# Expert value table of a PEER layer: half of its columns gathered, half streamed through a full weight matrix

## The chip, the cores and the metric

One NeuronCore of a Trainium2 chip runs the whole program. The metric is the time of one launch on the device in microseconds. Engines are named as in the profile: PE (TensorE), DVE (VectorE), ACT (ScalarE), POOL (GpSimd), SP (SyncE).

## What is computed

A layer of a streaming encoder for 256 tokens of width 2048: a token-mixing sub-layer (state-space branch and latent attention), then the PEER sub-layer, which the change is about. For each token and each of 8 heads, 16 of 16,384 experts are chosen; expert e is row e of `peer_u` and row e of `peer_v`, 2048 float32 (8 KB) each.

```python
q = jnp.dot(h, w_q).reshape(b, s, PEER_HEADS, 2, PEER_HALF)
s1 = jnp.einsum('bshd,kd->bshk', q[:, :, :, 0], keys_1)   # 128 keys
s2 = jnp.einsum('bshd,kd->bshk', q[:, :, :, 1], keys_2)
v1, i1 = lax.top_k(s1, PEER_TOPK)                         # 16
v2, i2 = lax.top_k(s2, PEER_TOPK)
# top 16 of the 16 x 16 sums; expert = i1 * 128 + i2; gate = softmax
u = jnp.take(u_table, e_blk, axis=0)
act = jax.nn.gelu(jnp.einsum('td,ted->te', h_blk, u), approximate=False)
v = jnp.take(v_table, e_blk, axis=0)
return jnp.einsum('te,ted->td', g_blk * act, v)
```

The result is scaled by `1 + gate2`, added to `ALPHA * x1` and normalised.

## The kernel before

The 256 tokens are two blocks of 128 tokens, one token on each partition. Up to about 1625 us of the trace the program streams weight matrices from SP through TensorE; in the last of these stages (`wq`, lines 1787 to 1817) DVE also finds the experts of head 0 of block 0 (`top_sides`, `top_pairs`, `top_experts`, lines 1756 to 1785). Then comes the stage `all`, the rest of the program.

Its unit is a group: one head of one block, 16 in all. A group has 32 gathers, 16 of `peer_u` and then 16 of `peer_v`. One gather (line 1993) is an indirect DMA that POOL issues: it fetches one table row for each of the 128 tokens, 128 x 8 KB or 1.05 MB, into one of the 8 slots of `rrow`. Row r goes to slot r mod 8, and POOL issues it once the user of row r - 8 is done with it (`row_used`, `row_used_pe`). All 32 gathers of a group wait for `expert_ready`, which DVE raises when it has written the group's 16 indices in `eid` (line 1784).

On DVE the order within a group (line 1832 on) is written out by hand:

```python
for e in range(TOPK):                 # 16 rows of peer_u: dots
    row = use_row(r0, e, i_sem)
    last = V.tensor_tensor_reduce(row, row, h2[:, b, :], ...)
top_sides(head + 1); top_pairs(1 - k); top_experts(1 - k)   # experts of the NEXT group
# gate, gelu -> wgt; 4 diagonal matrices for TensorE
# 12 rows of peer_v: ps += row * wgt      (4 rows go to TensorE)
```

So the experts of group g + 1 are found between the u rows and the v rows of group g. ACT supplies `gex` (exponential, line 1257) and `gel` (gelu, line 1267). The v rows are summed in PSUM: 12 of 16 by DVE into `ps` (line 1859), 4 of 16 by TensorE (line 929) as a matmul of a diagonal weight matrix `diag` with the row into `aux`. After 8 groups a block is finished (lines 1873 to 1880: both sums, gate, residual, layer norm) and stored by SP (line 541); block 1 follows.

Of the kernel before, what the change touches and what calls it, by code (L numbers as in the profile page):

```python
# [15 lines left out]
ds = bass.ds  # L16
# [42 lines left out]


# [24 lines left out]
def constants():  # L85

    c = np.zeros((P, C_ALL), np.float32)
# [9 lines left out]
    c[:, C_EPS] = EPS  # L97
    return c
# [29 lines left out]
def build(nc, a, out, stop="all"):  # L128
    ctx = ExitStack()
    with ctx:  # L130
# [49 lines left out]
        gate1, shift2, scale2, gate2 = (adabc[:, j, :] for j in range(4))  # L180
# [80 lines left out]
        ln2 = at("ln2", 174 * KB, [P, 2, D])  # L261
# [15 lines left out]
        tsel = pk("tsel", 6, [P, 2, TOPK])  # L277
        tval = pk("tval", 7, [P, 2, TOPK])
        eidf = pk("eidf", 8, [P, TOPK])
        eid = pk("eid", 9, [P, 2, TOPK], U32)  # L280
# [5 lines left out]
        wgt = pk("wgt", 15, [P, 2, TOPK])  # L286
        diag = acc[:, 0, :].rearrange("p (j n k) -> p j n k", j=2, n=2)
        fin = at("fin", 192 * KB, [P, D])
# [111 lines left out]
        diag_ready = sem("diag_ready")  # L400
        row_used_pe = sem("row_used_pe")
        sums_read = sem("sums_read")
        ln2_in = sem("ln2_in")
# [24 lines left out]
        ada_rows = nc.dram_tensor("ada_rows", (1, ADA_ALL * W), F32, kind="Internal").ap()  # L428

# [13 lines left out]


        PE_ROWS = tuple(TOPK + e for e in (3, 7, 11, 15))
        NPE, NDVE = len(PE_ROWS), 2 * TOPK - len(PE_ROWS)

        def rows_done(r, pe):

            n = r // (2 * TOPK) * NPE + sum(x <= r % (2 * TOPK) for x in PE_ROWS)  # L450
            return n if pe else r + 1 - n
# [5 lines left out]
        def _(sp_):  # L457
# [11 lines left out]
            sp_.dma_start(con[:, :], a["consts"]).then_inc(con_in, 16)  # L469
# [67 lines left out]
            if on("all"):  # L537
                for b in range(BLK):

                    sp_.wait_ge(fin_ready, b + 1)  # L540
                    sp_.dma_start(out[0, b * P:(b + 1) * P, :], fin[:, :]).then_inc(out_done, 16)
                sp_.wait_ge(out_done, 16 * BLK)
# [3 lines left out]
        def _(pe):  # L546
# [49 lines left out]
            pe.sem_inc(row_used_pe, NPE)  # L596
# [316 lines left out]
            if on("all"):  # L913
                pe.wait_ge(score_a, 4)
                pe.wait_ge(score_v, 4)
                for b in range(BLK):
                    if b:
                        pe.wait_ge(sums_read, 1)

                    def pair(i, first):  # L920
                        for k in range(2):
                            head = PEER_HEADS * b + k
                            for j, x in enumerate(PE_ROWS):
                                r = head * 2 * TOPK + x
                                pe.wait_ge(diag_ready, i * 4 + (head * 2 + j // 2 + 1))
                                pe.wait_ge(row_full[r % ROWS],
                                           i * (16 * 4 * TOPK // ROWS) + 16 * (r // ROWS + 1))
                                for n in range(4):
                                    last = mm(aux[:, n, :], diag[:, j // 2, j % 2, :],  # L929
                                              rrow[:, r % ROWS, n * W:n * W + W], start=(first and k == 0 and j == 0),  # L930
                                              stop=False, skip_group_check=True)
                                last.then_inc(row_used_pe, 1)

                    pair(0, True)
                    with pe.Fori(1, 4) as i:
                        pair(i, False)
# [3 lines left out]
        def _(act):  # L940
# [272 lines left out]
            if on("h2"):  # L1213
# [12 lines left out]
                for b in range(BLK):  # L1226
                    for q in range(4):
# [3 lines left out]
                            .then_inc(h2_hi_ready, 1)  # L1231
            if on("wq"):
# [16 lines left out]
            if on("all"):  # L1249

                act.wait_ge(score_v, 4)
                act.wait_ge(score_a, 4)
                for b in range(BLK):

                    def gate(n_expr, k):
                        act.wait_ge(top_ready, n_expr)
                        F(gex[:, k, :], tval[:, k, :], ACT.Exp, bias=ngm[:, k:k + 1], accum_out=gsum[:, k:k + 1])\
                            .then_inc(gate_exp, 1)

                    if b == 0:  # L1260
                        gate(1, 0)

                    def pair(i, last_one):
                        for k in range(2):

                            act.wait_ge(row_used, i * (2 * NDVE) + (ROWS + (PEER_HEADS * b + k) * NDVE + TOPK))
                            F(gel[:, k, :], dots[:, k, :], ACT.Gelu).then_inc(gelu_ready, 1)  # L1267
                            if not (last_one and k == 1):
                                gate(i * 2 + (PEER_HEADS * b + k + 2), 1 - k)

                    with act.Fori(0, 4 - b) as i:
                        pair(i, False)
                    if b:
                        pair(3, True)
                    norm_root(b + 5)
# [3 lines left out]
        def _(dve):  # L1279
# [412 lines left out]
            if on("mix"):  # L1692
# [5 lines left out]
                dve.wait_ge(ada_in_ready, 16 * 4)  # L1698
# [39 lines left out]
            if on("wq"):  # L1738
# [32 lines left out]
                def top_experts(k):  # L1771
# [5 lines left out]
                    for s in range(2):  # L1777
# [4 lines left out]
                        link(V.tensor_reduce(tsel[:, s, :], onehot[:, :, :], AX_X, ALU.add))  # L1782
                    link(V.scalar_tensor_tensor(eidf[:, :], tsel[:, 0, :], float(KEYS), tsel[:, 1, :], ALU.mult, ALU.add))
                    V.tensor_copy(eid[:, k, :], eidf[:, :]).then_inc(expert_ready, 1)  # L1784
                    V.tensor_scalar(ngm[:, k:k + 1], tval[:, k, 0:1], -1.0, None, ALU.mult).then_inc(top_ready, 1)

                def use_row(r0, e, n_trip):

                    r = r0 + e
                    dve.wait_ge(row_full[r % ROWS], n_trip * (16 * 4 * TOPK // ROWS) + 16 * (r // ROWS + 1))  # L1790
# [9 lines left out]
                for s in range(4):  # L1800
                    for q in range(4):
# [10 lines left out]
                        if (s, q) == (3, 0):  # L1812
                            top_experts(0)
# [4 lines left out]
            if on("all"):  # L1818
                dve.wait_ge(ln2_in, 32)
                dve.wait_ge(qT_a, 4)  # L1820
                for b in range(BLK):
                    link(V.memset(psf, 0.0))
                    dve.wait_ge(score_a, 4)
                    base = b * PEER_HEADS * 2 * TOPK

                    def pair(i, last_one, i_sem):
                        for k in range(2):
                            r0 = base + k * 2 * TOPK

                            for e in range(TOPK):  # L1830
                                row = use_row(r0, e, i_sem)
# [14 lines left out]
                            head = PEER_HEADS * b + k  # L1846
                            for j in range(2):

                                dve.wait_ge(row_used_pe, i_sem * (2 * NPE) + (NPE + head * NPE - 2 + 2 * j))
                                for n in range(2):  # L1850
# [193 lines left out]
```

## Time and profile before

| | us |
|---|---|
| median of 3 runs | 3003.13 |
| lowest, highest | 2998.79, 3005.52 |
| the profiled execution | 3004.59 |
| its span, first to last instruction | 3002.7 |
| DVE busy | 2353.8 (78%) |
| PE busy | 1807.9 (60%) |
| POOL busy | 961.5 (32%) |
| DMA queue q0 (gathers and others from POOL) | 614.51 MB, 50.9% of 16 engines' span |

The page divides the span in 40 slices of 75 us. The stage `all` takes slices 22 to 40. Durations below come from the profiled execution. In a row of the groups, the first number after the bar is the busy time in us, then the mean of one in ns, then the idle time before them with what ended it. "DMA share" is the mean busy share of the 16 DMA engines.

### The profile page before, as it was taken

What the parts mean: (1) busy time and instruction counts of PE and PEld (TensorE: products, weight loads), DVE (VectorE), ACT (ScalarE), POOL (GpSimd) and SP (SyncE); (2) the same over time, 40 slices, a digit from 0 to 9 for tenths busy, and PEclk for the clock granted to TensorE, in tenths of its full rate; (3) what the DMA queues carried; (4) which work ended last, traced back from release to release, by engine and by line L of the source; (5) the groups of instructions that cost most, each with busy time, mean ns of one, the idle gap of its engine ahead of it and who ended that gap; (6) DMA issues with size and microseconds to landing.
All of it is one profiled execution on the core that took longest, in us unless ns stands there. A gap on an engine that the chain in (4) does not pass through costs nothing.

```text
span 3002.7 us, 31625 instructions
## 1 busy us (share of the span) xinstructions
PE 1807.9 (60%) x10880; PEld 1498.1 (50%) x10880; DVE 2353.8 (78%) x2564; ACT 683.0 (23%) x712; POOL 961.5 (32%) x727
## 2 busy tenths in 40 slices
PE   4689999999999999998886223212122222212322
PEld 3589998888888889997786111001001110000111
DVE  7757677788877874444657999998999989989997
ACT  1144442344444444333342000000000000000000
POOL 0000011222222220000003555655663555556652
PEclk9799999999999999999988665565665655556556
DMA  8746568655555554655536999999998999999996
GB/s 339 285 173 214 205 222 299 223 209 203 207 207 197 196 189 177 239 182 210 182 141 244 386 402 403 403 397 400 420 400 321 380 403 393 403 404 400 398 404 265
DMA packets 135095, 880.07 MB, mean 293 GB/s; under 512 B 15416, under 2 KB 20144, under 8 KB 36944
## 3 DMA queue, kind: packets, MB, share of 16 engines
q0 software_dynamic: 93600, 614.51, 50.9%
q1 hardware_dynamic: 39792, 263.69, 24.2%
q8 instruction: 66, 1.08, 0.1%
q10 hardware_dynamic: 1600, 0.49, 0.1%
q14 instruction: 37, 0.30, 0.0%
HBM read 876.50 MB, written 2.13 MB: 293 GB/s over the span
## 4 chain that ended last, share of the span: by engine, by line
PE 40%; DVE 27%; DMA 14%; issue 10%; POOL 5%; ACT 3%; DVEq 0%; ACTq 0%; POOLq 0%
DMA rrow<-in_peer_u,eid 10%; PE ps L585 9%; DVE ps L1859 9%; PE ps L587 9%; PE ps L586 9%; POOL rrow L1993 5%; DVE rrow L1832 3%; DMA rrow<-in_peer_v,eid 3%; DVE wlo L1288 2%; ACT whi L949 2%; PE ps L565 2%; DVE acc L1337 2%; PE ps L567 2%; PE ps L566 2%; PE aux L929 1%
## 5 line engine op out<-in xcount | busy, mean ns | idle before, releaser
L929 PE MATMUL aux<-rrow,acc 128*128 128x512 f32 x512 | 337.0, 825 | 1018.7 <-DVE acc L1852 774.6
L1288 DVE TENSOR_TENSOR wlo<-raw,whi 128x2048 fp32r<-128x2048 f32 x216 | 510.7, 2366 | 374.2 <-ACT whi L949 365.4
L929 PEld LDWEIGHTS aux<-rrow,acc 128*128 128x128 f32 x512 | 133.8, 272 | 1221.3 <-issue 971.3
L1832 DVE CUSTOM_DVE_ANT_0 rrow<-rrow,h 128x2048 f32<-128x2048 f32 x256 | 584.0, 2292 | 61.0 <-DMA rrow<-in_peer_u,eid 52.4
L949 ACT ACTIVATE whi<-raw 128x2048 fp32r<-128x2048 f32 x216 | 412.8, 1913 | 704.6 <-PE ps L587 478.6
L1993 POOL DMA_INDIRECT rrow<-in_peer_u,eid x256 | 416.5, 1627 | 310.2 <-DVE eid L1784 90.3
L1993 POOL DMA_INDIRECT rrow<-in_peer_v,eid x256 | 356.0, 1391 | 358.0 <-DVE ps L1859 292.3
L1859 DVE SCALAR_TENSOR_TENSOR ps<-rrow,wgt,ps 128x2048 f32<-128x2048 f32 x192 | 452.2, 2355 | 14.4 <-DMA rrow<-in_peer_v,eid 6.8
L585 PE MATMUL ps<-h_hi,whi 128*128 128x256 f32 (+1 forms) x1568 | 453.3, 289 | 5.8 <-DVE wlo L1288 4.4
L587 PE MATMUL ps<-h_hi,wlo 128*128 128x256 f32 (+1 forms) x1568 | 443.5, 283 | 0.0
L586 PE MATMUL ps<-h_lo,whi 128*128 128x256 f32 (+1 forms) x1568 | 443.5, 283 | 0.0
L1898 POOL DMA_DIRECT2D ada_in<-in_p_ada x128 | 69.3, 541 | 749.1 <-DVEq L1438 599.8
L585 PEld LDWEIGHTS ps<-h_hi,whi 128*128 128x128 f32 (+1 forms) x1568 | 299.1, 191 | 18.9 <-issue 10.5
L586 PEld LDWEIGHTS ps<-h_lo,whi 128*128 128x128 f32 (+1 forms) x1568 | 299.1, 191 | 4.0 <-issue 3.8
L587 PEld LDWEIGHTS ps<-h_hi,wlo 128*128 128x128 f32 (+1 forms) x1568 | 299.0, 191 | 0.0
L1267 ACT ACTIVATE gel<-dots 128x16 f32<-128x16 f32 x16 | 3.4, 216 | 1048.9 <-DVE dots L1832 1048.9
L1337 DVE SCALAR_TENSOR_TENSOR acc<-ada_in,csil,acc 128x512 f32<-128x512 f32 x240 | 205.6, 857 | 20.0 <-DMA ada_in<-in_p_ada 5.9
L565 PE MATMUL ps<-whi,h_hi 128*128 128x512 f32 x320 | 135.9, 425 | 54.1 <-DVE wlo L1288 54.1
L585 PE MATMUL ps<-yT_hi,whi 128*128 128x256 f32 x512 | 144.9, 283 | 0.0
L586 PE MATMUL ps<-yT_lo,whi 128*128 128x256 f32 x512 | 144.9, 283 | 0.0
L587 PE MATMUL ps<-yT_hi,wlo 128*128 128x256 f32 x512 | 144.9, 283 | 0.0
L566 PE MATMUL ps<-whi,h_lo 128*128 128x512 f32 x320 | 131.6, 411 | 0.0
(312 smaller groups left out, 3056.5 us busy)
## 6 DMA issues: line engine op xcount, KB each, us to landing
raw<-in_p_in SPq DMA_DIRECT2D x104, 1024.0 KB, 4.9
ada_in<-in_p_ada POOLq DMA_DIRECT2D x128, 512.0 KB, 5.2
ada_in<-in_p_ada SPq DMA_DIRECT2D x32, 1024.0 KB, 9.7
raw<-in_p_so SPq DMA_DIRECT2D x32, 1024.0 KB, 4.9
raw<-in_p_mo SPq DMA_DIRECT2D x16, 1024.0 KB, 7.1
raw<-in_p_bc SPq DMA_DIRECT2D x16, 1024.0 KB, 4.9
raw<-in_p_mix SPq DMA_DIRECT2D x16, 1024.0 KB, 4.9
raw<-in_p_pq SPq DMA_DIRECT2D x16, 1024.0 KB, 4.8
```

The source lines that it names most:

```text
L565: mm(outs[b], x_hi[:, k, t], hi[:, kc, 0:width], start=(k == 0), stop=False)
L566: mm(outs[b], x_lo[:, k, t], hi[:, kc, 0:width], start=False, stop=False)
L585: mm(o, wh, x_hi[:, k, :], start=(k == 0 and first), stop=False, skip_group_check=True)
L586: mm(o, wh, x_lo[:, k, :], start=False, stop=False, skip_group_check=True)
L587: last = mm(o, wl, x_hi[:, k, :], start=False, stop=(k == klast), skip_group_check=True)
L929: last = mm(aux[:, n, :], diag[:, j // 2, j % 2, :], rrow[:, r % ROWS, n * W:n * W + W], start=(first and k == 0 and j == 0), stop=False, ...
L949: F(whi[:, n % 2, :, 0:cols_], raw[:, n % 4, :, 0:cols_], ACT.Copy).then_inc(hi_ready, 1)
L1288: V.tensor_tensor(wlo[:, n % 2, :, 0:cols_], raw[:, n % 4, :, 0:cols_], whi[:, n % 2, :, 0:cols_].bitcast(F32), ALU.subtract).then_inc(lo_ ...
L1337: last = V.scalar_tensor_tensor(acc_, tile[:, kc, :], csil[:, k:k + 1], acc_, ALU.mult, ALU.add)
L1832: last = V.tensor_tensor_reduce(row, row, h2[:, b, :], 1.0, 0.0, ALU.mult, ALU.add, dots[:, k, e:e + 1])
L1859: V.scalar_tensor_tensor(psf, row, wgt[:, k, e:e + 1], psf, ALU.mult, ALU.add)\
L1993: G.indirect_dma_start(out=rrow[:, r % ROWS, :], out_offset=None, in_=a[table][0], in_offset=bass.IndirectOffsetOnAxis(ap=eid[:, k, e:e + ...
```

## The change

The stage `all` is split in two passes over all 16 groups, and the 2048 columns of `peer_v` in two halves.

* Pass 1 (before.py's loop, `pair`) handles only `peer_u`: 16 rows of a group, then the experts of the next group, then the weights of this group, into a table `w_all` of 256 columns that keeps all weights. The indices go to `eid_all`, the two key numbers of each expert to `sides`.
* Columns 1024 to 2047 of `peer_v` (input `p_vg`, laid out apart) are gathered in a second pass: 256 gathers of 128 x 4 KB, each added by DVE into `ps` (`add_row`). There are 8 slots `vrow`. None of them goes to TensorE.
* Columns 0 to 1023 (input `p_vd`) are not gathered. A matrix of weights is built with one column per expert for every token: `wt[b][k1, k2, t]`, 128 x 128 x 128 float32 for each block, which holds the weight where token t has chosen expert (k1, k2) and zero elsewhere. For each token it is the product of two one-hot matrices over the token's 128 selections, one of them scaled by the weights: 32 steps of 4 tokens per block. The one-hots of block 0 are made by ACT during the second half of pass 1 (`one_hots`), those of block 1 by DVE after pass 1, each step followed by one `add_row`. ACT copies each product from PSUM to `wt` (`weights_out`).
* Then the whole left half of the table is read by SP in 64 units of 1.05 MB through 4 buffers (`vden`), 8 float32 matmuls of 128x512 each, into `aux`.
* Both blocks are finished together at the end. `x1`, whose place the matrices take, is stored in DRAM (ACT's queue) and read back, with gate2 and the last norm's rows. The loads of `ln2` leave the start of the stage, and one of four broadcast loads of `adabc` is replaced by a small one.

```diff
@@ DVE, pass 1
                             if not (last_one and k == 1):
-                                top_sides(i * 2 + (PEER_HEADS * b + k + 1))
+                                top_sides(group + 1)
                                 top_pairs(1 - k)
-                                top_experts(1 - k)
+                                top_experts(1 - k, group + 1)
...
-                            link(V.scalar_tensor_tensor(wgt[:, k, :], gel[:, k, :], st[:, 48 + k:49 + k],
-                                                        gex[:, k, :], ALU.mult, ALU.mult))
...
-                            for n, e in enumerate(mine):
-                                row = use_row(r0 + TOPK, e, i_sem)
...
-                                V.scalar_tensor_tensor(psf, row, wgt[:, k, e:e + 1], psf, ALU.mult, ALU.add)\
-                                    .then_inc(row_used, 1)
+                            V.scalar_tensor_tensor(w_all[:, ds(group * TOPK, TOPK)], gel[:, k, :], st[:, 48 + k:49 + k],
+                                                   gex[:, k, :], ALU.mult, ALU.mult).then_inc(w_ready, 1)
@@ DVE, after pass 1
+                for n in range(OHB):
+                    if n >= 2:
+                        dve.wait_ge(wt_done, OHB + n - 1)
+                    o = oh[1][:, n % 2]
+                    t4 = slice(n * OHT, n * OHT + OHT)
+                    link(V.tensor_tensor(o, niota.unsqueeze(1).unsqueeze(1).broadcast_to([P, 2, OHT, P]),
+                                         selT[:, 0:2, t4].unsqueeze(3).broadcast_to([P, 2, OHT, P]), ALU.is_equal))
+                    V.tensor_tensor(o[:, 1], o[:, 1], selT[:, 2, t4].unsqueeze(2).broadcast_to([P, OHT, P]), ALU.mult)\
+                        .then_inc(oh_ready, 1)
+                    add_row(n)
+                for r in range(OHB, BLK * SEL):
+                    add_row(r)
@@ POOL
+                for r in range(BLK * SEL):
+                    if r % TOPK == 0:
+                        pool.wait_ge(expert_ready, r // TOPK + 1)
...
+                    pool.wait_ge(row_used, r + 1)
+                    gather(rrow[:, r % ROWS, :], a["peer_u"][0], r).then_inc(row_full[r % ROWS], 16)
+                for r in range(BLK * SEL):
+                    if r < ROWS:
...
+                        pool.wait_ge(row_used, ROWS + BLK * SEL - ROWS + r // 2 + 1)
+                    else:
+                        pool.wait_ge(vrow_used, r - ROWS + 1)
+                    gather(vrow[:, r % ROWS, :], a["p_vg"], r).then_inc(vrow_full[r % ROWS], 16)
@@ SP
+                for u in range(NVU):
+                    if u < 4:
...
+                        sp_.wait_ge(row_used, ROWS + BLK * SEL - 4 + u + 1)
+                    else:
+                        sp_.wait_ge(vden_used, u - 3)
+                    if u == 3:
...
+                        sp_.wait_ge(wt_done, BLK * OHB)
+                    sp_.dma_start(vden[:, u % 4], a["p_vd"][u * P:(u + 1) * P, :].rearrange("p (q n) -> p q n", q=2))\
+                        .then_inc(vden_full[u % 4], 16)
@@ PE
+                pe.wait_ge(wt_read, BLK * OHB)
+                for u in range(NVU):
+                    pe.wait_ge(vden_full[u % 4], vden_before[u % 4] + 16 * (u // 4 + 1))
+                    for q in range(2):
+                        for b in range(BLK):
+                            for n in range(DV // W):
+                                last = mm(aux[:, 2 * b + n, :], wt_column(b, 2 * u + q),
+                                          vden[:, u % 4, q, n * W:n * W + W],
+                                          start=(u == 0 and q == 0), stop=(u == NVU - 1 and q == 1))
+                    last.then_inc(vden_used, 1)
```

How the instructions stand in the program. First DVE at the border of the last two groups, before (`eid` gets the indices, `ps` the sums; "ISA" with `dots` is one u row):

```order
L1782 TENSOR_REDUCE tsel<-onehot 128x16
L1783 SCALAR_TENSOR_TENSOR eidf<-tsel 128x16
L1784 CAST eid<-eidf 128x16
L1785 TENSOR_SCALAR ngm<-tval 128x1
L1841 RECIPROCAL st<-gsum 128x1
L1843 SCALAR_TENSOR_TENSOR wgt<-gel,st,gex 128x16
L1852 TENSOR_SCALAR acc<-con,wgt 128x128 x4
L1859 SCALAR_TENSOR_TENSOR ps<-rrow,wgt,ps 128x2048 x12
L1832 ISA rrow,dots<-rrow,h_72 128x2048
L1832 ISA dots 128x1
```

Between the indices and the next group's first u row stand 12 v rows. The same place of the change (`acc` is now the store of `eid_all` and `w_all`):

```order
L1884 TENSOR_REDUCE sides<-onehot 128x16
L1885 SCALAR_TENSOR_TENSOR eidf<-sides 128x16
L1887 CAST acc<-eidf 128x16
L1888 TENSOR_SCALAR ngm<-tval 128x1
L1939 RECIPROCAL st<-gsum 128x1
L1941 SCALAR_TENSOR_TENSOR acc<-gel,st,gex 128x16
L1930 ISA rrow,dots<-rrow,h_72 128x2048
L1930 ISA dots 128x1
```

The v rows are gone from there: the u rows that need the indices of line 1887 come next. They stand behind the last group, on DVE, where the one-hots of block 1 (`oh`) begin:

```order
L1939 RECIPROCAL st<-gsum 128x1
L1941 SCALAR_TENSOR_TENSOR acc<-gel,st,gex 128x16
L1973 TENSOR_TENSOR oh_165<-cos_60,selT 128x1024
L1975 TENSOR_TENSOR oh_165<-oh_165,selT 128x512
L1957 TENSOR_SCALAR ps<-vrow,acc 128x1024
L1973 TENSOR_TENSOR oh_165<-cos_60,selT 128x1024
L1975 TENSOR_TENSOR oh_165<-oh_165,selT 128x512
L1960 SCALAR_TENSOR_TENSOR ps<-vrow,acc,ps 128x1024
```

Each v row is now 1024 wide, and the first 32 of 256 alternate with one step of one-hots each.

## Rows read from the trace of the kernel before

**Rows 1.** The page: the span in 40 equal slices (75 us each).
```profile
DVE  7757677788877874444657999998999989989997
...
DMA  8746568655555554655536999999998999999996
```

**Rows 2.** The page: costliest groups of instructions, with idle before them.
```profile
L1832 DVE CUSTOM_DVE_ANT_0 rrow<-rrow,h 128x2048 f32<-128x2048 f32 x256 | 584.0, 2292 | 61.0 <-DMA rrow<-in_peer_u,eid 52.4 <-issue 8.1 <-DVE ps L1822 0.5
...
L1993 POOL DMA_INDIRECT rrow<-in_peer_v,eid x256 | 356.0, 1391 | 358.0 <-DVE ps L1859 292.3
L1859 DVE SCALAR_TENSOR_TENSOR ps<-rrow,wgt,ps 128x2048 f32<-128x2048 f32 x192 | 452.2, 2355 | 14.4 <-DMA rrow<-in_peer_v,eid 6.8
```

**Rows 3.** Timeline of DVE: start us, us, instruction [idle <-releaser].
```profile
1624.63 1.76 DVE L1822 MEMSET ps<- 128x2048 f32 x1 [0.42 <-issue]
1626.67 2.29 DVE L1832 CUSTOM_DVE_ANT_0 rrow<-rrow,h 128x2048 f32<-128x2048 f32 x1 [0.27 <-DVE ps L1822]
...
1662.07 0.29 DVE L1758 COPY scur<-score 128x256 f32 x1
...
1674.52 0.17 DVE L1784 CAST eid<-eidf 128x16 uint32<-128x16 f32 x1
...
1676.02 28.66 DVE L1859 SCALAR_TENSOR_TENSOR ps<-rrow,wgt,ps 128x2048 f32<-128x2048 f32 x12
1705.60 2.32 DVE L1832 CUSTOM_DVE_ANT_0 rrow<-rrow,h 128x2048 f32<-128x2048 f32 x1 [0.92 <-DMA rrow<-in_peer_u,eid]
```

**Rows 4.** Timeline of DVE and of POOL, the stage's first indices and gather.
```profile
1609.27 0.17 DVE L1784 CAST eid<-eidf 128x16 uint32<-128x16 f32 x1
...
1610.45 2.15 POOL L1993 DMA_INDIRECT rrow<-in_peer_u,eid  x1 [90.30 <-DVE eid L1784]
```

**Rows 5.** Windows: us, POOL busy, PEclk, DMA share, GB/s.
```profile
1610.00:1612.00 2.00, 1.55 (x1) 1.00 0.00 0
1612.00:1614.00 2.00, 1.55 (x2) 1.00 0.50 82
...
1675.00:1678.00 3.00, 0.00 (x0) 0.50 0.18 68
...
1681.00:1684.00 3.00, 0.97 (x2) 1.00 0.91 330
```

**Rows 6.** All gathers by tile eid: us from issue to landing.
```profile
DMA to landing us min/median/max: 8.9/14.0/17.9
```

**Rows 7.** DMA issues by line: KB each, median us to landing.
```profile
raw<-in_p_in SPq DMA_DIRECT2D x104, 1024.0 KB, 4.9
```

**Rows 8.** Windows again, a stretch of mixed loads and one of gathers.
```profile
500.00:510.00 10.00, 2.11 (x4) 1.00 0.93 334
1700.00:1750.00 50.00, 37.54 (x21) 0.58 1.01 420
```

**Rows 9.** Groups by form, DVE: busy us, mean ns.
```profile
L1357 DVE SCALAR_TENSOR_TENSOR ada_acc<-ada_in,csil,ada_acc 128x1024 f32<-128x1024 f32 x52 | 66.8, 1285 | 9.7 <-DMA ada_in<-in_p_ada 8.1
...
L1652 DVE TENSOR_TENSOR yg<-yg,zs 128x1024 f32<-128x1024 f32 x8 | 9.8, 1226 | 0.3
...
L1577 DVE TENSOR_TENSOR premix<-ps,premix 128x512 f32 x8 | 5.1, 682 | 0.0
```

**Rows 10.** Timeline of weight loads of L929, each before one 128x512 matmul.
```profile
1678.85 0.34 PEld L929 LDWEIGHTS aux<-rrow,acc 128*128 128x128 f32 x1 [0.52 <-issue]
1679.70 0.34 PEld L929 LDWEIGHTS aux<-rrow,acc 128*128 128x128 f32 x1 [0.52 <-issue]
...
1681.34 0.19 PEld L929 LDWEIGHTS aux<-rrow,acc 128*128 128x128 f32 x1 [0.24 <-issue]
1681.77 0.19 PEld L929 LDWEIGHTS aux<-rrow,acc 128*128 128x128 f32 x1 [0.24 <-issue]
```

**Rows 11.** Timeline of DVE at the end.
```profile
2979.25 2.29 DVE L1873 COPY fin<-aux 128x2048 f32<-128x2048 f32 x1 [5.69 <-PE aux L929]
...
2995.71 2.29 DVE L1880 TENSOR_TENSOR fin<-fin,ln 128x2048 f32<-128x2048 f32 x1
```

More of the change, by code:

```diff
@@ L179, in build @@
         adabc = at("adabc", 78 * KB, [P, 4, D])
[L180 removed]
+        gate1, shift2, scale2 = (adabc[:, j, :] for j in range(3))
         premix = at("premix", 110 * KB, [P, DC, SEQ])
@@ L916, in _ @@
                 for b in range(BLK):
[L917 to L932, printed above, removed]
@@ L934, in _ @@
-                    pair(0, True)
-                    with pe.Fori(1, 4) as i:
-                        pair(i, False)
+                    pe.wait_ge(w_ready, PEER_HEADS * (b + 1))
+                    for k in range(3):
+                        src = w_all[:, b * SEL:(b + 1) * SEL] if k == 2 else sides[:, k, b * SEL:(b + 1) * SEL]
+                        last = nc.tensor.transpose(aux[:, 2, k * P:k * P + P], src, ident)
+                    last.then_inc(sel_turned, 1)
+                    for n in range(OHB):
+                        m = b * OHB + n
+                        pe.wait_ge(oh_ready, m + 1)
+                        if m >= 2:
+                            pe.wait_ge(wt_read, m - 1)
+                        for t in range(OHT):
+                            last = mm(aux[:, n % 2, t * P:t * P + P], oh[b][:, n % 2, 0, t, :], oh[b][:, n % 2, 1, t, :],
+                                      start=True, stop=True)
+                        last.then_inc(wt_done, 1)
@@ L1252, in _, with gate @@
                 act.wait_ge(score_a, 4)
-                for b in range(BLK):
[L1255 to L1275, printed above, removed]
+                def gate(n_expr, k):
+                    act.wait_ge(top_ready, n_expr)
+                    F(gex[:, k, :], tval[:, k, :], ACT.Exp, bias=ngm[:, k:k + 1], accum_out=gsum[:, k:k + 1])\
+                        .then_inc(gate_exp, 1)
@@ new lines, in _ @@
+                gate(1, 0)
+                with act.Fori(0, 4) as i:
+                    for k in range(2):
+                        gelu(i * (2 * TOPK) + (ROWS + (k + 1) * TOPK), k)
+                        gate(i * 2 + (k + 2), 1 - k)
+                act.wait_ge(iota_in, 16)
+                act.wait_ge(x1_stored, 16 * BLK)
+                turned(0)
+                act.wait_ge(selT_ready, 1)
+                per = OHB // PEER_HEADS
+                for g in range(PEER_HEADS):
+                    for n in range(per * g, per * g + per):
+                        one_hots(n)
+                        if n:
+                            weights_out(0, n - 1)
+                    gelu(ROWS + (PEER_HEADS + g + 1) * TOPK, g % 2)
+                    if g < PEER_HEADS - 1:
+                        gate(PEER_HEADS + g + 2, 1 - g % 2)
@@ new lines, in _ @@
+                dve.wait_ge(vden_used, NVU)
+                for b in range(BLK):
+                    S.step(V.scalar_tensor_tensor(fin[:, b, 0:DV], gate2b[:, 0:DV], 1.0,
+                                                  aux[:, 2 * b:2 * b + 2, :].rearrange("p a n -> p (a n)"), ALU.add, ALU.mult))
+                S.wait()
+                for b in range(BLK):
+                    S.step(V.scalar_tensor_tensor(fin[:, b, 0:DV], x1b[:, b, 0:DV], ALPHA, fin[:, b, 0:DV],
+                                                  ALU.mult, ALU.add))
@@ new lines, in gather @@
+                def gather(dst, table, r):
+                    pool.sem_inc(held, 1)
+                    return G.indirect_dma_start(
+                        out=dst, out_offset=None, in_=table,
+                        in_offset=bass.IndirectOffsetOnAxis(ap=eid_all[:, r:r + 1], axis=0))
+                for r in range(BLK * SEL):
+                    if r % TOPK == 0:
+                        pool.wait_ge(expert_ready, r // TOPK + 1)
+                    if r in (0, 1):
+                        pool.wait_ge(lo_ready, U_END + 3 + r)
+                    if r == 4:
+                        pool.wait_ge(pe_used, U_END + 2)
+                    pool.wait_ge(row_used, r + 1)
+                    gather(rrow[:, r % ROWS, :], a["peer_u"][0], r).then_inc(row_full[r % ROWS], 16)
```

228 lines of the change are left out of this document (142 added, 86 removed).

## Prediction

> **What bounds the kernel now.** I read the page's slices first. From slice 23 on both DVE and the DMA engines stand at 8 or 9 tenths, but for the last slice of DMA [rows 1], so in the stage `all` two resources are near their limit together and the order of the work decides. The costliest groups say which ends last: the 256 u rows waited 61.0 us in all, nearly all of it for their gathers, and the 192 v rows 14.4 us; POOL, at 1.4 us per v gather, itself waited for DVE to free slots [rows 2]; in a stretch with nothing but gathers the DMA share is 1.01 at 420 GB/s [rows 8]. One gather of 1.05 MB at 420 GB/s takes 2.5 us, 32 of them 80 us. The timeline of DVE shows a group's cycle. The last u row of the first group ends at about 1662.1, finding the next group's experts lasts until 1674.7, then 12 v rows run until 1704.7, and the next u row starts at 1705.6 after a wait of only 0.92 us [rows 3]. That is what I look at most: the gathers of the next u rows are issued while DVE adds v rows, so when DVE gets there the rows have landed. The v rows cover the refill of the pipeline; where there is none to issue, the engines run dry, as in 1675 to 1678 with a DMA share of 0.18 [rows 5]. The stage is bound by bytes, and its order keeps the bytes flowing.
>
> **The change, part by part.**
>
> *Start.* The memset of 1.76 us before the first u row goes, so that row starts 2.0 us earlier, at 1624.7 [rows 3]. The first group keeps its 35.4 us (1626.7 to 1662.1) since its index table is ready long before: its last u row ends at 1660.1.
>
> *Pass 1.* The order of DVE shows indices, weights, and then at once the u rows that need these indices; POOL may issue none of them before `expert_ready`, and it has no v rows to issue in between. So nothing is in flight while DVE finds experts, and each border of two groups is serial:
> - experts, 1662.1 to 1674.7: 12.5 us [rows 3];
> - from the indices written (1609.44) to the issue (1610.45): 1.0 us [rows 4];
> - issue to landing: the fastest of all gathers took 8.9 us, the median 14.0 behind a full queue [rows 6]. With an empty queue no data moves for the first 2 us [rows 5]. I take 9.0; bounds 4.9, a direct load of the same size [rows 7], and 11.9, short of the median;
> - then 15 more rows at 2.5 us each, 37.5 us: DVE needs 2.29 per row [rows 2], the DMA engines 2.5, and 8 slots were enough for this pace before;
> - the last row on DVE, 2.3 us.
>
> Sum 62.3 us per group; 15 of them after the first give 934 us: pass 1 ends at 2594. The weights of a group (0.5 us) lie inside the wait for the gather. ACT's one-hots of block 0 are 4 steps per group; even at 10 us each they take 40 of the 62 us, and TensorE is idle otherwise. I cost both at nothing; without this cover up to 8 x 40 us would show.
>
> *Build of block 1.* The last weights, three transposes and ACT's copies come first, 4 us. A step is one DVE operation of 1024 columns (1.23 us), one of 512 (0.68) and one v row of 1024 into PSUM (1.29) [rows 9], with gaps 3.35 us; 32 steps are 107 us, and 2 us more until the last product is copied. I take DVE as the bound, since TensorE's four 128-wide products and ACT's copy of 512 columns are each under 2 us. It ends at 2707. Bounds: 96 us (no gaps), and 186 us if the two buffers make the three engines take turns. During it the DMA engines get only 32 half rows to fetch and 3 units of the stream; the unit with number 3 is held until all products are done.
>
> *Stream and second pass.* Left are 61 units of 1.05 MB and 216 half rows of 0.52 MB (32 are used, 8 landed): 64.0 + 113.2 = 177 MB. DVE needs 216 x 1.3 = 281 us. TensorE does 8 matmuls per unit; the weight loads before them are 0.85 us apart at the beginning of a burst and 0.43 later [rows 10], and the granted clock goes from 0.50 to 1.00 meanwhile (1.2 to 2.4 GHz) [rows 5], so a unit is 6.8 or 3.4 us, 61 of them 417 or 209 us. DMA: 420 GB/s for gathers of 8 KB rows [rows 8] gives 422 us; a stretch in which loads with 4 KB rows made up about six tenths of the bytes, as here, reached 334 GB/s at a share of 0.93, that is 359 GB/s when full [rows 8], 494 us. I take 400 GB/s, since that stretch was not full and the share there holds waiting: 443 us. DMA is the longest of the three at either clock, so the clock costs nothing here. It ends at 3150.
>
> *Tail.* Before: 23.5 us from the first closing operation (2979.25) to the end of the span [rows 11]. Now both blocks close together: the last v row (1.3), eight operations of 1024 columns (10), statistics of both (5.6), a root (1), four of 2048 (9.4), and 4.7 from the last operation to the end of the span as before: 32 us. Span 3182.
>
> *Saved, for comparison.* The left half of the v rows was 268 MB of gathers and is 67 MB now, the right half is again 134 MB in place of 268: 537 MB become 470. At 420 GB/s the 67 MB are 160 us. Against this stand 15 borders: each replaces no wait with about 22 us in which nothing lands, 330 us, and the build with its half-empty queue, some 60 us. The store and reload of x1, four megabytes, lie beside other work.
>
> *Sum.* 3182 against a span of 3002.7 is +179 us. The profiled execution took 3004.6, 1.5 us above the median, so I forecast 3003.1 + 179 = **3182 us**.
>
> *A rule weighed against a row.* Every border stands on the 9.0 us from issue to landing, from the row of 8.9 [rows 6]. The Trainium skill, DMA: Bandwidth & Descriptors, the section on the anatomy of one DMA, gives a fixed cost of about 2.0 us plus the bytes over 436 GB/s for a DMA from GpSimd. By that rule an estimate for one gather is 4.4 us, and the sum would be 3113. The trace disagrees for gathers: none of 512 landed under 8.9.
>
> **The rivals.**
>
> *The refill is short.* After an idle spell nothing else is in the queue, which no row before shows cleanly (the fastest row had three more behind it). If a gather then lands in 4.9 us, like a direct load [rows 7], each border is 4.1 us shorter, 15 x 4.1 = 62: 3120 us. Against it: the first 2 us without data [rows 5] are POOL's and stay. The Trainium skill's rule above is this case, at 3113.
>
> *The gathers take the engines, the stream comes last.* If the half rows get all they can use (one per 1.30 us, 403 GB/s), they end after 281 us, and the 61 units follow alone, bound by TensorE: 209 us at the high clock. 490 in place of 443: 3229 us. At the low clock it would be 417: 3437 us. Rows 10 speak against the latter, since the clock rose within a burst.
>
> *The build takes turns.* 186 in place of 107 us: 3261 us. For it: two buffers, low clock; against: each engine's part is short.
>
> *The other side, faster.* If the gathers of a group run ahead of its border (the index wait does not hold them where I think, or the landing falls into DVE's own work), a border costs DVE's time alone: 12.5 + 16 x 2.21 + 0.4 = 48.3 us. 15 x 14.0 = 210 us less: 2972 us. It decides as soon as more than 12 of the 22 us of a border are covered, since 179 / 15 is 12. Against it: the wait stands before every sixteenth gather, and the indices are written after the last u row of the group before.
>
> **How the numbers follow.** The forecast's mechanism 0.60; short refill 0.11; gathers first 0.13, and at the low clock 0.03; build in turns 0.08; run ahead 0.04; 0.01 that several of my bounds fall on the low side together and it comes out even. What a measurement of this kernel can tell from no change is 0.2%, 6 us. So faster 0.04, same 0.01, slower 0.95. Range: the low end takes the short refill and a little of the faster DMA (3120 - 10); the high end takes the slow DMA (3182 + 51) and the build in turns (3261) with a margin for both in part: 3110 to 3290 us.
>
> **What would show it.** The groups should show u rows waiting about 10 us for a gather once per group, 150 us or more in all, and the slices of pass 1 a DMA share near 0.7. The first u row of the second group should start about 23 us after the last of the first. Pass 1 should end near 2594, the build near 2707, with 3.3 to 3.5 us per step; the stream should run at 380 to 420 GB/s with a share near 1.0, and DVE and PE both with idle time there. I am wrong if the u rows do not wait at the borders; if the stream alone is left at the end for over 50 us; or if the v pass moves under 350 GB/s.

## The result, and the profile after

The changed kernel takes **3139.49 us** (median of 4 runs, 3135.28 to 3140.03) against 3004.27 us (4 runs, 2998.79 to 3005.52) for the kernel before on the same chip: a ratio of 1.0451, with a 95% interval of 1.0433 to 1.0469, 135 us slower. The forecast was 3182 us, with 3110 to 3290 as its range. The profiled execution has a span of 3137.3 us.

The slices and the costliest groups of the page of the changed kernel (the span in 40 slices of 78.4 us; then line, engine, operation, tiles, count | busy us, mean ns | idle before, releaser):

```profile
DVE  6766687888777854445668788788788789666567
...
PEclk9799999999999999999885555555555555999998
DMA  8746677666565546555366676677577596999996
...
L1930 DVE CUSTOM_DVE_ANT_0 rrow<-rrow,h 128x2048 f32<-128x2048 f32 x256 | 585.7, 2292 | 147.0 <-DMA rrow<-in_peer_u,acc 146.5
L2094 POOL DMA_INDIRECT rrow<-in_peer_u,acc x256 | 452.8, 1769 | 681.7 <-DVE acc L1887 601.8
...
L1960 DVE SCALAR_TENSOR_TENSOR ps<-vrow,acc,ps 128x1024 f32<-128x1024 f32 x254 | 327.1, 1288 | 162.7 <-DMA vrow<-in_p_vg,acc 145.2
...
L989 PE MATMUL aux<-vden,wt 128*128 128x512 f32 x512 | 244.0, 599 | 5.3 <-DMA vden<-in_p_vd 4.5
...
L989 PE MATMUL aux<-vden,wt1a 128*128 128x512 f32 x384 | 181.3, 595 | 0.0
```

In slices 21 to 32, which hold pass 1, the DMA engines stand at 5 to 7 tenths; before, they stood at 8 or 9 in the stage `all` but for its first and last slice [rows 1]. The 256 u rows wait 146.5 us for their gathers where all their idle time before was 61.0 us [rows 2], and POOL sits idle for 601.8 us in all, in 16 stretches, until DVE has written the indices (L1887). In slices 35 to 39 both the DMA engines and the TensorE clock stand at 9: the stream with the second pass.

A border of two groups in the timeline of DVE and then of POOL (start us, us, instruction, [idle <-releaser]):

```profile
1656.08 2.29 DVE L1930 CUSTOM_DVE_ANT_0 rrow<-rrow,h 128x2048 f32<-128x2048 f32 x1
...
1658.29 0.29 DVE L1858 COPY scur<-score 128x256 f32 x1
...
1671.19 0.17 DVE L1887 CAST acc<-eidf 128x16 f32 x1
...
1671.65 0.24 DVE L1941 SCALAR_TENSOR_TENSOR acc<-gel,st,gex 128x16 f32 x1 [0.15 <-DVE st L1939]
1677.68 2.29 DVE L1930 CUSTOM_DVE_ANT_0 rrow<-rrow,h 128x2048 f32<-128x2048 f32 x1 [5.80 <-DMA rrow<-in_peer_u,acc]
...
1680.92 2.29 DVE L1930 CUSTOM_DVE_ANT_0 rrow<-rrow,h 128x2048 f32<-128x2048 f32 x1 [0.94 <-DMA rrow<-in_peer_u,acc]
```
```profile
1672.20 0.93 POOL L2094 DMA_INDIRECT rrow<-in_peer_u,acc  x1 [28.51 <-DVE acc L1887]
```

The last u row of group 1 ends at 1658.3, experts run to 1671.3, POOL issues at 1672.20, and the first u row of group 2 starts at 1677.68: 19.4 us between two u rows, in which DVE works for experts only. Before, the next u row came 0.92 us after the last v row [rows 3]. The first u row of the last group starts at 2513.50, 14 groups later, so one group takes (2513.50 - 1677.68) / 14 = 59.7 us.

Windows of the changed kernel (us, busy of PE, PEld, DVE, ACT, POOL with counts, granted clock, DMA share, GB/s): the border, the flow of u gathers, the build of block 1, and the stream beside the second pass.

```profile
1660.00:1671.00 11.00, 0.00 (x0) 0.00 (x0) 8.40 (x32) 0.00 (x0) 0.00 (x0) 0.50 0.00 1
1673.00:1675.00 2.00, 0.00 (x0) 0.00 (x0) 0.00 (x0) 0.16 (x1) 1.39 (x3) 0.50 0.57 119
1678.00:1690.00 12.00, 0.00 (x0) 0.00 (x0) 10.41 (x9) 0.00 (x0) 10.47 (x6) 0.50 1.01 420
2556.00:2656.00 100.00, 66.53 (x257) 57.00 (x258) 96.98 (x98) 21.43 (x65) 36.51 (x33) 0.50 0.65 209
2760.00:2860.00 100.00, 100.00 (x235) 44.27 (x234) 64.02 (x51) 0.00 (x0) 46.98 (x51) 1.00 1.02 414
```

At the border 1 GB/s moves for 11 us; after it the flow is at once 420 GB/s at a share of 1.01. In the build DVE is the busy engine (97 of 100 us). In the stream TensorE is busy for 100 of 100 us **at the high clock** and the DMA engines are full too. So two resources are at their limit in that stage, where the prediction had one. In the window 2657.5 to 3107 TensorE is busy for 444.09 of 449.50 us, and 408 GB/s move.

How the forecast's stations came out:

| step | forecast | measured |
|---|---|---|
| first u row of the stage | 1624.7 | 1622.9 |
| experts at a border | 12.5 us | 13.0 us |
| indices to issue | 1.0 us | 0.8 us |
| issue to first u row on DVE | 9.0 us | **5.5 us** |
| pace of the rows behind it | 2.5 us | 2.49 us |
| one group | 62.3 us | 59.7 us |
| end of pass 1 | 2594 | 2555.7 |
| last weights to first one-hot | 4 us | 2.4 us |
| one build step; all of them, up to the first product of the stream | 3.35, 109 us | 3.05, 99.5 us |
| stream with second pass | 443 us | 450 us (2657.5 to 3107) |
| TensorE per unit, high clock | 3.4 us | **6.83 us** |
| tail | 32 us | 30 us |

### The profile page after: what moved, and what is told of

Same layout as the page of the kernel before. It is cut to its first block, busy times and chain, and to the rows that moved or that the text cites. A ratio compares the mean times of both kernels' runs of the same rounds, so it can differ in the third digit from the quotient of the medians.

```text
span 3137.3 us, 33782 instructions
## 1 busy us (share of the span) xinstructions
PE 2045.8 (65%) x11910; PEld 1672.6 (53%) x11910; DVE 2258.9 (72%) x2624; ACT 871.6 (28%) x1227; POOL 893.8 (28%) x725
## 4 chain that ended last, share of the span: by engine, by line
PE 37%; DMA 19%; DVE 18%; issue 13%; POOL 10%; ACT 3%; DVEq 0%; ACTq 0%; POOLq 0%
DMA vrow<-in_p_vg,acc 11%; POOL rrow L2094 9%; PE ps L638 9%; PE ps L640 9%; PE ps L639 9%; DMA rrow<-in_peer_u,acc 6%; DVE ps L1960 3%; DVE wlo L1388 2%; ACT whi L1005 2%; DVE acc L1437 2%; PE ps L618 2%; PE ps L619 2%; PE ps L620 2%; DVE rrow L1930 1%; DVE oh L1973 1%
## 5 line engine op out<-in xcount | busy, mean ns | idle before, releaser
L1930 DVE CUSTOM_DVE_ANT_0 rrow<-rrow,h 128x2048 f32<-128x2048 f32 x256 | 585.7, 2292 | 147.0 <-DMA rrow<-in_peer_u,acc 146.5
L2094 POOL DMA_INDIRECT rrow<-in_peer_u,acc x256 | 452.8, 1769 | 681.7 <-DVE acc L1887 601.8
L1960 DVE SCALAR_TENSOR_TENSOR ps<-vrow,acc,ps 128x1024 f32<-128x1024 f32 x254 | 327.1, 1288 | 162.7 <-DMA vrow<-in_p_vg,acc 145.2
L980 PE MATMUL aux<-oh 128*128 128x128 f32 x512 | 132.8, 441 | 406.6 <-ACT oh L1349 373.5
L980 PEld LDWEIGHTS aux<-oh 128*128 128x128 f32 x512 | 114.0, 328 | 425.7 <-ACT oh L1349 383.0
L2094 POOL DMA_INDIRECT vrow<-in_p_vg,acc x256 | 253.3, 989 | 304.5 <-DVE ps L1960 233.7
L989 PE MATMUL aux<-vden,wt 128*128 128x512 f32 x512 | 244.0, 599 | 5.3 <-DMA vden<-in_p_vd 4.5
L989 PE MATMUL aux<-vden,wt1a 128*128 128x512 f32 x384 | 181.3, 595 | 0.0
L989 PEld LDWEIGHTS aux<-vden,wt 128*128 128x128 f32 x512 | 98.1, 192 | 129.0 <-issue 122.6
```

Of the source, the lines that this page charges most:

```text
L980: last = mm(aux[:, n % 2, t * P:t * P + P], oh[b][:, n % 2, 0, t, :], oh[b][:, n % 2, 1, t, :], start=True, stop=True)
L989: last = mm(aux[:, 2 * b + n, :], wt_column(b, 2 * u + q), vden[:, u % 4, q, n * W:n * W + W], start=(u == 0 and q == 0), stop=(u == NVU - ...
L1930: last = V.tensor_tensor_reduce(row, row, h2[:, b, :], 1.0, 0.0, ALU.mult, ALU.add, dots[:, k, e:e + 1])
L1960: last = V.scalar_tensor_tensor(o, row, w, o, ALU.mult, ALU.add)
L2094: return G.indirect_dma_start(out=dst, out_offset=None, in_=table, in_offset=bass.IndirectOffsetOnAxis(ap=eid_all[:, r:r + 1], axis=0))
```

## Experiments

The kernel before took 3001.70 us (7 runs) on the chip of the first four kernels and 3003.12 us (7 runs) on that of the last four, 3004.27 us beside the change: times of different chips can be compared to within 0.1%. e2 to e5 have a single time each; the four times of the other kernels lie within 4 to 9 us of each other.

### e1_ahead: the experts of the next group before the u rows of this one

```diff
+if not (last_one and k == 1):
+    top_sides(group + 1)
+    top_pairs(1 - k)
+    top_experts(1 - k, group + 1)
 for e in range(TOPK):
     row = use_row((PEER_HEADS * b + k) * TOPK, e, i_sem)
     ...
-if not (last_one and k == 1):
-    top_sides(group + 1)
-    ...
```

> The changed kernel, with the experts of the next group found before the u rows of a group instead of after them, so that its gathers can be issued while DVE works on the rows. Theory 'border' (15 borders at which the gathers wait for the indices and nothing lands): a group costs DVE's time alone, 12.5 us for the experts, 35.4 for 16 rows and some 0.7 for the wait for gelu that the experts hid; pass 1 lasts about 765 us in place of 933, the kernel about 2971 us, which is faster than both. Rival 'bytes' (pass 1 is slow because the gathers themselves run slower in it, whatever the order): less than 20 us gained, above 3115 us.

Measured **2980.09 us** (4 runs, 2973.66 to 2982.17), ratio to before 0.9921, interval 0.9905 to 0.9938: 159 us under the change, and 0.8% under the kernel before, a small difference but outside the noise. Nothing is computed more or less; DVE only does the same 13 us at a moment when the indices of the rows that it needs next are known, so that up to 8 of their gathers, one per slot, are on their way or landed. From the costliest groups of e1, and a window over its pass 1 and one over its stream:

```profile
L1934 DVE CUSTOM_DVE_ANT_0 rrow<-rrow,h 128x2048 f32<-128x2048 f32 x256 | 567.9, 2287 | 1.8 <-DMA rrow<-in_peer_u,acc 1.6
```
```profile
1625.00:2010.00 385.00, 0.00 (x0) 0.00 (x0) 357.75 (x576) 25.47 (x40) 231.07 (x126) 0.50 0.84 339
2500.00:2940.00 440.00, 434.88 (x1004) 192.34 (x1004) 278.66 (x217) 1.94 (x3) 202.29 (x216) 0.99 1.02 412
```

The u rows wait 1.6 us in all, in place of 146.5. A group takes 49.0 us (its experts start at 1625.57, the next ones at 1674.58), and DVE is now what pass 1 is bound by, busy for 357.75 of 385 us while the DMA share is 0.84. 15 borders times (59.7 - 49.0) are 160 us, and the time fell by 159. The last stage did not change: its first product starts at 2501.5 in place of 2657.5, and the products take 449 us as before.

### e2_index_wait: the same order, but the wait for the indices one group earlier

```diff
-pool.wait_ge(expert_ready, r // TOPK + 1)
+pool.wait_ge(expert_ready, max(r // TOPK, 1))
-gather(rrow[...], a["peer_u"][0], r).then_inc(...)
+gather(rrow[...], a["peer_u"][0], r if r < TOPK else r - TOPK).then_inc(...)
```

> The changed kernel in its own order, but each group gathers the u rows with the indices of the group before it (the first group with its own), so that POOL no longer waits for new indices; the same bytes are moved and the values are those of other experts. Theory 'border': the wait for indices is the whole loss, so a group costs 12.5 + 35.4 us of DVE, 15 x 11.6 = 174 us less: about 2965 us, and the u rows wait for gathers under 20 us in all. Rival 'bytes': above 3115 us. Rival 'order' (the position of the experts' instructions matters in another way than through the indices): e1 gains and this one does not.

Measured **2972.69 us**. DVE's order is that of the change, and only POOL's wait and the column of indices differ. The timeline of DVE in e2 at the same border:

```profile
1670.90 0.17 DVE L1887 CAST acc<-eidf 128x16 f32 x1
...
1671.35 0.23 DVE L1941 SCALAR_TENSOR_TENSOR acc<-gel,st,gex 128x16 f32 x1 [0.15 <-DVE st L1939]
1671.50 2.29 DVE L1930 CUSTOM_DVE_ANT_0 rrow<-rrow,h 128x2048 f32<-128x2048 f32 x1
```

The u row follows the indices after 0.6 us with no wait; all 256 u rows of e2 waited 2.0 us together. So the cost of a border is that the gathers *cannot be issued* before the indices, and not where the experts stand on DVE.

### e3_before_bare: the kernel before, its experts moved behind the v rows

```diff
-if not (last_one and k == 1):
-    top_sides(i * 2 + (PEER_HEADS * b + k + 1))
-    top_pairs(1 - k)
-    top_experts(1 - k)
 ...
     V.scalar_tensor_tensor(psf, row, wgt[:, k, e:e + 1], psf, ALU.mult, ALU.add)...
+if not (last_one and k == 1):
+    top_sides(i * 2 + (PEER_HEADS * b + k + 1))
+    ...
```

> The kernel before, with the experts of the next group found after the v rows instead of between u and v rows: all else is equal. Theory 'border': the cover that the v rows gave is gone, each border adds the experts (12.5), the issue (1.0) and the first landing (5.4) to a group that else is bound by 32 gathers at 2.5 us: 98.7 us per group in place of 83.4, 15 x 15.3 = 230 us more: about 3234 us. Rival 'bytes': the DMA engines decide in either order, under 20 us more: about 3020 us.

Measured **3193.4 us**, 191.7 more than before: the kernel before can be given the same borders, without a stream, a one-hot or a product. From its groups, and the first u row behind a border in the timeline of its DVE:

```profile
L1832 DVE CUSTOM_DVE_ANT_0 rrow<-rrow,h 128x2048 f32<-128x2048 f32 x256 | 584.4, 2292 | 144.4 <-DMA rrow<-in_peer_u,eid 143.9
...
L1855 DVE SCALAR_TENSOR_TENSOR ps<-rrow,wgt,ps 128x2048 f32<-128x2048 f32 x192 | 452.2, 2355 | 119.8 <-DMA rrow<-in_peer_v,eid 105.8
```
```profile
1716.85 2.29 DVE L1832 CUSTOM_DVE_ANT_0 rrow<-rrow,h 128x2048 f32<-128x2048 f32 x1 [6.53 <-DMA rrow<-in_peer_u,eid]
```

Its u rows wait 143.9 us, as in the change (146.5). The price is 12.8 us per border, where 15.3 were expected. The border itself came as expected: from the end of the last v row (1697.85) to the next u row (1716.85) it is 19.0 us, where 12.5 + 1.0 + 5.4 = 18.9 had been put. The difference lies elsewhere: an ordinary group takes 97 us in place of the 98.7 expected, and the border between the two blocks, where block 0 is finished in any order, costs 4 us only (112.1 against 107.9 from one group's first u row to the next).

### e4_stream_alone: 224 of the 256 half rows left out

```diff
+VROWS = 32
-for r in range(OHB, BLK * SEL):
+for r in range(OHB, VROWS):
     add_row(r)
-dve.wait_ge(vrow_used, BLK * SEL)
+dve.wait_ge(vrow_used, VROWS)
-for r in range(BLK * SEL):
+for r in range(VROWS):
```

This kernel gathers and adds only the first 32 half rows; the rest of the right half of the output is missing.

> The changed kernel with only the first 32 of the 256 half-row gathers of peer_v (the other 224 and their additions are left out), so that the stream of 64 units is alone after the build. Theory 'products' (the stream is bound by TensorE: 8 float32 matmuls of 512 columns, each two passes of 0.427 us, 6.83 us per unit): the stream still takes about 440 us, the kernel about 3130 us. Rival 'bytes' (my prediction: the stream is bound by the DMA engines and TensorE needs 3.4 us per unit at the high clock): 61 units alone at 3.4 us or less, some 210 us, the kernel about 2900 us.

Measured **3124.64 us**: 117 MB less to move and 15 us gained. A window of its stream, columns as above:

```profile
2800.00:2900.00 100.00, 100.00 (x235) 44.27 (x234) 0.00 (x0) 0.00 (x0) 0.00 (x0) 1.00 0.43 150
```

The DMA engines are at 0.43, DVE and POOL are idle, and TensorE is busy all the time at the high clock. Its stream runs from 2657.5 to 3099. So TensorE alone takes 441 us for it, and the sentence of the prediction that DMA is the longest of the three at either clock was wrong.

### e5_half_products: only one block's half of the products

```diff
-for b in range(BLK):
+for b in range(1):
     for n in range(DV // W):
         last = mm(aux[:, 2 * b + n, :], wt_column(b, 2 * u + q), ...)
```

Here the products of block 1 are left out, so its left half is not computed.

> The changed kernel with only block 0's products in the stream: TensorE does 4 of the 8 matmuls of each unit, 3.4 us; the left half of block 1's output is left out. Theory 'two limits' (TensorE at 437 us and the DMA engines at 177 MB / 414 GB/s = 428 us stand side by side in the last stage): the DMA engines still set it, the kernel about 3120 us. Rival 'TensorE alone' (the DMA engines had room): the stage falls to what DVE needs for 224 half rows, 290 us, the kernel about 2980 us.

Measured **3153.97 us**: half the work of TensorE in the stream, and 14 us *slower*. Two windows of it, the second after the stream:

```profile
2700.00:2860.00 160.00, 138.77 (x298) 54.33 (x297) 54.63 (x43) 0.00 (x0) 40.19 (x43) 0.94 1.02 416
2960.00:3060.00 100.00, 0.00 (x0) 0.00 (x0) 92.48 (x73) 0.00 (x0) 67.30 (x72) 0.50 0.99 376
```

With the products cheaper, the stream takes more of the DMA engines: only 43 half rows come in 160 us (51 in 100 us in the change), and the last product is over at 2921. So in the change it is the slow products that hold the stream back and leave the rest of the DMA engines to the gathers. What is left is gathers alone, and there DVE is busy for 92.48 of 100 us and 376 GB/s move, 1.37 us per half row. From the end of pass 1 to the last addition e5 takes 566 us and the change 552, so the 14 us lie in this stage. Neither theory had this: not the faster product (2980) and not the bytes (3120). With e4 it says that relieving TensorE alone gains nothing here, and relieving the DMA engines and DVE, with the products left as they are, gains 15 us.

### e6_build_bare: no additions in the build

```diff
-    add_row(n)
-for r in range(OHB, BLK * SEL):
+for r in range(BLK * SEL):
     add_row(r)
```

> The changed kernel with the 32 additions of half rows moved from between the 32 build steps of block 1 to behind them. The build falls from 98 us to about 66 (DVE 1.9 us a step, TensorE's four products 2.1 us at the low clock), and 24 more half rows are left for the stage after it. Theory 'two limits': 194 MB at 414 GB/s, 469 us, now set that stage, so the kernel gains 32 and loses about 20: about 3125 us. Rival 'TensorE alone': the stream starts 32 us earlier and all of it is kept: about 3107 us. Rival of my prediction's kind, where the build's additions are free: 3139 us, no change.

Measured **3148.22 us** (4 runs, 3143.97 to 3152.66), ratio to before 1.0486, interval 1.0468 to 1.0505; the change had 1.0451, 1.0433 to 1.0469. All three expectations (3125, 3107, 3139) were below it. The two intervals just touch, so the 9 us between the medians are hardly clear of noise, and in the two profiles 4 us of the difference arise before the build (pass 1 ends at 2559.6 against 2555.7). What the profile does show is that nothing was gained. The build became shorter by over a third (62.0 us in place of 99.5 from the first one-hot to the first product of the stream; in 2560 to 2620 the granted clock was 0.93, where the change had 0.50), and the stream started 33.5 us earlier (2624.0 against 2657.5) and ended as much earlier (the last product starts at 3071.0 against 3105.6). But the 32 additions were then behind it. Windows of e6, columns as above, of the build and of the gathers alone after the stream, and then the end of its DVE timeline:

```profile
2560.00:2620.00 60.00, 37.47 (x243) 31.36 (x243) 56.89 (x63) 20.45 (x63) 1.39 (x2) 0.93 0.21 83
3079.00:3116.00 37.00, 0.00 (x0) 0.00 (x0) 34.18 (x28) 0.00 (x0) 20.52 (x22) 0.50 0.91 359
```
```profile
3069.45 48.62 DVE L1960 SCALAR_TENSOR_TENSOR ps<-vrow,acc,ps 128x1024 f32<-128x1024 f32 x35
3118.18 2.35 DVE L1982 SCALAR_TENSOR_TENSOR fin<-gate2b,ps 128x1024 f32<-128x1024 f32 x2
```

The last 35 additions take 48.62 us, 1.39 us each, with nothing else to do on DVE, and the closing operations begin at 3118.2 in place of 3107.6. So the additions inside the build were no cost that could be saved: they are work for DVE and bytes for the DMA engines that have to be done anyway, and the build is a place where they fit.

### e7_ahead_bare and e8_ahead_half: both together, and half of it

e7 is e1 with the edit of e6. e8 is e1 with an addition in every second build step:

```diff
-    add_row(n)
-for r in range(OHB, BLK * SEL):
+    if n % 2:
+        add_row(n // 2)
+for r in range(OHB // 2, BLK * SEL):
     add_row(r)
```

> e1 (experts ahead) and e6 (bare build) together. The two touch different stages, so the gains should add: e1's 2980 us less what e6 gained against the changed kernel, about 2966 us. If the gathers' new start at the end of pass 1 disturbs the build, it stays at 2980.

> e1 with an addition in every second build step: the build lasts about 80 us, 14 to 16 half rows are done in it, and the stage after it moves 186 MB, 449 us, beside TensorE's 442 us. By 'two limits' that is the balance: 80 + 449 = 529 against 66 + 469 = 535 for the bare build and 98 + 450 = 548 for e1: about 2961 us, some 5 us under e7. By 'TensorE alone' it is slower than e7 by 14 us.

e7 took **2988.04 us** (2983.24 to 2990.68; ratio 0.9957, 0.9940 to 0.9974), e8 **2983.56 us** (2980.74 to 2984.85; 0.9937, 0.9920 to 0.9954), e1 had 0.9921, 0.9905 to 0.9938. The removal costs 8 us here as it did alone (3148.22 - 3139.49 = 9; as ratios 0.9957 - 0.9921 and 1.0486 - 1.0451, 0.4% both times), so the two edits add up, and half of it cannot be told from none. The gain that I expected of a better balance, 14 to 20 us, did not come. In the traces the last addition ends at 2950.6 in e1, 2951.7 in e7 and 2952.3 in e8, though the stream of products ends at 2950.6, 2904.4 and 2926.6: a shorter build moved the end of the products and not the end of the gathers. e1 has the lowest time of the kernels here that compute the whole, and e8 cannot be told from it.

## Why the prediction was right, and where it was not

**The direction and the mechanism** were right: the v rows had covered the refill of the pipeline, and without them each border is serial. e1, e2 and e3 show it from three sides: take the borders away and 159 us go (e1), take the wait alone away and 167 go (e2), put the borders into the kernel before and 192 come (e3).

**Where the 135 us come from.** The borders cost 160 us, by e1. Without them the change would be a small gain: 2980.09 against 3001.70 on the same chip, 22 us. The prediction's own comparison named both sides, 160 us of bytes saved against 15 borders and a build, but put the borders at 330 us, twice what e1 shows: of its 22 us per border DVE needs 13 for the experts wherever they stand. The price that it gave for gathers that run ahead of the border, 48.3 us per group and 2972 us, is what e1 and e2 then measured (49.0 us per group and 2980; 48.8 and 2973).

**Issue to landing, 9.0 us: the term that was mis-sized.** It was 5.5 us, at 1672.20 to 1677.68 and again at the next border (issue 1731.76, u row 1737.3). The bounds held it (4.9 to 11.9), the value I took did not. I had rested it on the fastest landing in the view of all gathers, 8.9 us [rows 6], and argued that none of 512 was shorter. That reading was wrong: the view has a landing time for a part of the gathers only, 128 of the 512 in either kernel. The same view of the changed kernel over the window 1671:1680, the first six gathers behind a border:

```profile
L2094 POOL DMA_INDIRECT rrow<-in_peer_u,acc x6: 932/937/2374, 1672.2 to 1678.4; - x6
...
DMA to landing us min/median/max: 11.3/11.9/12.5
```

The first of the six was read 5.5 us after its issue, and the least of the view is 11.3. Asked for each of the first four alone, it gives no landing at all. The 11.3 belongs to the fifth (issued 1677.16), whose u row starts at 1688.47, and the 12.5 to the sixth (issued 1678.40), whose u row starts at 1690.96. So where the view has a value it agrees with the reader to within 0.1 us, and of the first gather behind a border it says nothing; neither did the row of before. What a reader waits must be taken from the reader's own row. That error alone is 15 x 3.5 = 52 us of the sum, more than the whole miss of 43; smaller errors the other way hid a part of it.

By the rule of the Trainium skill, DMA: Bandwidth & Descriptors, on the anatomy of one DMA (2.0 us plus the bytes over 436 GB/s), an estimate for this gather is 4.4 us. The measured 5.5 us lie 1.1 above it and 3.5 under my term, so the case that I gave as *the refill is short*, at 3120, was the better account of this step, and I weighed the rule against a row that holds no gather of this kind: the prediction's sentence that the trace disagrees was not shown.

**TensorE's price, a step that was wrong.** I took the spacing of weight loads in a burst [rows 10] as the time of one matmul; the heading of those rows says the same, and it is wrong in the same way. The trace has 512 + 384 + 128 = 1024 records of L989 where the program has 64 x 2 x 2 x 2 = 512 matmuls: a float32 matmul leaves two records, each with a weight load of its own. The timeline of weight loads of the changed kernel, where the clock rises (in the build before it was 0.50, in the stream 1.00):

```profile
2661.97 0.34 PEld L989 LDWEIGHTS aux<-vden,wt1a 128*128 128x128 f32 x1 [0.52 <-issue]
2662.82 0.23 PEld L989 LDWEIGHTS aux<-vden,wt1a 128*128 128x128 f32 x1 [0.52 <-issue]
...
2664.15 0.19 PEld L989 LDWEIGHTS aux<-vden,wt 128*128 128x128 f32 x1 [0.24 <-issue]
2664.58 0.19 PEld L989 LDWEIGHTS aux<-vden,wt 128*128 128x128 f32 x1 [0.24 <-issue]
```

Two records of 0.427 us are 0.85 us per matmul at the high clock and 1.7 at the low one; a unit of 8 is 6.83 us and 64 of them 437. It happened to be as long as what I had for DMA (443), so the stage's time came out while its reason was half wrong. e4 shows the error in full: the rival named there, with the price of 3.4 us, stood at 2900, and the kernel took 3124.64. The count of L929 could have told it before the change: 512 records for 16 x 4 x 4 = 256 matmuls.

**DMA in the stream.** I took 400 GB/s between 359 and 420; it is 414, so rows of 4 KB among rows of 8 KB cost almost nothing, and the stretch at 359 [rows 8] was no bound for this stage; why it was slower was not tested. 177 MB and five closing loads of 1.05 MB, which I had left out, are 440 us at 414 GB/s. TensorE's 441 us (e4) and the DMA engines' 440 are the same length by chance, and the 450 us are either of them and a little more: one wait of TensorE for a unit, 4.5 us at 2974, is the only stop of over 1 us. The last product starts at 3105.6 and the last addition ends at 3107.5. DVE's 216 half rows at 1.3 us are 281 us, well under both. e4 and e5 show that relieving one of the two gives 15 us or nothing.

**The rest.** Experts 13.0 in place of 12.5 (+0.5 x 15), the start 2 us earlier, the build 9.5 us shorter (steps of 3.05, DVE without gaps), its entry 1.6 shorter, the tail 2 shorter, the stream 7 longer. The rivals *gathers first* and *build in turns* did not occur. e5 shows the opposite of the former: given a choice, the stream gets its share first and the gathers are left over. The low clock did occur in the build, at 0.50 with TensorE busy two thirds of the time, but DVE covered it.

**Still open.** Other splits than half and half were not run; with e1's order and two equal limits in the last stage, a third of the columns as a stream might be better or worse. e2 to e5 rest on one time and one trace each.

## What to carry to other kernels

When a loop is split and the second half moves away, ask what that half covered: here it hid the 13 us of index computation and the 6 us of refill of each next group, and the fix is to compute indices one group ahead, not to undo the split. Price a matmul by the number of records that one instruction leaves, and a wait by the row of the reader; before a minimum of a view is taken as a bound, ask for how many instructions the view has a value at all. Where a stage merges three engines, compute all three limits before choosing what to relieve: making one part shorter can push its work behind the stage (e6) or shift who gets the DMA engines (e5).

## What the chip did that I had not expected

- A float32 matmul with 512 columns takes 0.85 us at 2.4 GHz. The Trainium skill, TensorE: Matmul & The Clock Gate, on what each phase is for, says the throughput is one column per cycle, which would be an estimate of 0.21 us; for these float32 matmuls the trace disagrees by a factor of four.
- A queue of gathers that starts from nothing is at 420 GB/s six microseconds after the first issue (windows above: 119 GB/s from 1673 to 1675, 420 from 1678 on).
- When both wanted the DMA engines, direct loads with large rows from SP's queue pushed gathers from POOL's queue down to 43 half rows in 160 us, 141 GB/s of the 416 (e5).
